# Rotation tables of the state space built inside the second MLP's weight loop on GpSimd, in the attention's old query space

## The reference

```
mag = exp(lr * dt)
ar, ai = mag * cos(li * dt), mag * sin(li * dt)
...
_, _, xr, xi = lax.associative_scan(combine, (a_r, a_i, bu_r, bu_i), axis=1)
y = einsum('blgp,ghp->blgh', xr, c_re) - einsum('blgp,ghp->blgh', xi, c_im)
```

```
x = x + mod_x[5] * sqrelu_mlp(rms_norm(x, g) * (1 + mod_x[4]) + mod_x[3], mlp_w1, mlp_w2)
```

## Time and profile before

| | us |
|---|---|
| median of 3 timed runs | 2764.59 |
| lowest, highest | 2762.73, 2766.24 |
| the profiled execution, device time | 2760.31 |
| its span in the trace | 2758.5 |
| PE busy in the span | 2454.7 (89%) |
| GpSimd busy in the span | 1125.4 (41%) |

### The profile page before, as it was taken

One profiled execution on the slowest core, in us unless ns is written; L12 is line 12 of the kernel. 1 busy time (PEld: TensorE's weight loads), 2 busy tenths in 40 slices (PEclk: granted clock), 3 DMA queues, 4 the chain that ended last, 5 costly groups with the idle time before them and its releaser, 6 DMA issues.

```text
span 2758.5 us, 31907 instructions
## 1 busy us (share of the span) xinstructions
PE 2454.7 (89%) x11622; PEld 1975.0 (72%) x11622; DVE 1513.6 (55%) x2034; ACT 956.7 (35%) x1494; POOL 1125.4 (41%) x843
## 2 busy tenths in 40 slices
PE   5999768899999997679989999897878788899999
PEld 5888657788888886556768888676534465688887
DVE  6756756755555544988552122479379444452523
ACT  3312222512121224457552233443333343432322
POOL 1433003344444432358634444345764131344444
PEclk6999879999999998889999999999989899999999
DMA  5333103232333331321122323132200020232323
GB/s 223 115 102 127 39 8 115 84 114 101 112 111 102 114 99 39 102 54 41 56 77 92 99 92 96 62 108 84 92 0 0 31 73 27 69 107 91 99 92 107
DMA packets 68821, 231.68 MB, mean 84 GB/s; under 512 B 8048, under 2 KB 10992, under 8 KB 68592
## 3 DMA queue, kind: packets, MB, share of 16 engines
q1 hardware_dynamic: 68720, 230.35, 25.8%
HBM read 219.57 MB, written 2.10 MB: 80 GB/s over the span
## 4 chain that ended last, share of the span: by engine, by line
PE 57%; issue 15%; DVE 13%; POOL 10%; ACT 3%; DMA 1%; SPq 0%; POOLq 0%; DVEq 0%; ACTq 0%
PE PS L640 41%; POOL HL L517 9%; PE PS L658 6%; DVE RD L2242 2%; PE PS L677 1%; PE PS L609 1%; PE PS L901 1%; DVE ZZ L2396 1%; DVE SM L2226 1%; PE PS L1160 1%; PE PS L783 1%; PE PS L1042 1%; PE PS L1077 1%; DVE STATE L2081 1%; PE PS L786 1%
## 5 line engine op out<-in xcount | busy, mean ns | idle before, releaser
L517 POOL TENSOR_TENSOR HL<-RAW,HL 128x512 fp32r<-128x512 f32 x614 | 905.0, 1497 | 1502.3 <-ACT HL L1205 1502.0
L640 PE MATMUL PS<-HA,HL 128*128 128x512 f32 (+1 forms) x2592 | 557.3, 368 | 18.3 <-DVE V L2007 5.1
L640 PE MATMUL PS<-HID,HL 128*128 128x512 f32 (+1 forms) x2832 | 565.6, 362 | 0.0
L640 PE MATMUL PS<-HB,HL 128*128 128x512 f32 (+1 forms) x2592 | 542.8, 362 | 0.0
L640 PEld LDWEIGHTS PS<-HID,HL 128*128 128x128 f32 x2832 | 478.8, 188 | 85.4
L640 PEld LDWEIGHTS PS<-HA,HL 128*128 128x128 f32 x2592 | 444.4, 190 | 111.4 <-issue 32.3
L640 PEld LDWEIGHTS PS<-HB,HL 128*128 128x128 f32 x2592 | 442.8, 189 | 77.5
L1205 ACT ACTIVATE HL<-RAW 128x1024 fp32r<-128x1024 f32 x307 | 323.0, 1053 | 495.5 <-PE PS L640 385.5
L1859 DVE CUSTOM_DVE_ANT_0 ADJ<-ADA,CB 128x1024 f32<-128x1024 f32 x160 | 267.8, 1674 | 8.8 <-DVE X L1781 2.7
L1781 DVE SCALAR_TENSOR_TENSOR X<-PS,MOD,X 128x256 f32<-128x256 f32 (+1 forms) x120 | 75.7, 658 | 335.2 <-PE PS L640 317.1
L658 PE MATMUL PS<-HA,HL 128*128 128x256 f32 (+1 forms) x576 | 136.1, 399 | 69.6 <-DVE HA L1762 49.2
(11 more groups left out here) (372 smaller groups left out, 2779.1 us busy)
## 6 DMA issues: line engine op xcount, KB each, us to landing
RAW<-wstream SPq DMA_DIRECT2D x307, 512.0 KB, 3.5
ADA<-adastream SPq DMA_DIRECT2D x80, 512.0 KB, 3.6
EARLY<-adastream SPq DMA_DIRECT2D x16, 512.0 KB, 14.4
QB<-QH SPq DMA_DIRECT2D x32, 128.0 KB, 2.3
X<-x_in SPq DMA_DIRECT2D x8, 384.0 KB, 6.8
QC<-QL SPq DMA_DIRECT2D x16, 128.0 KB, 2.3
out<-X SPq DMA_DIRECT2D x8, 256.0 KB, 2.3
X<-mem SPq DMA_DIRECT2D x1, 1024.0 KB, 12.3
```

The source lines that it names most:

```text
L517: a = pool.tensor_tensor(HL[:, t % RING, 1, half], RAW[:, t % RAW_RING, half], HL[:, t % RING, 0, half].bitcast(F32), ALU.subtract)
L640: mm = pe.matmul(bank(t % 2, r), w[:, wp, k * P:(k + 1) * P], a[:, ap, lo:hi], start=(k == 0 and (wp, ap) == (0, 0)), stop=(k == nk - 1 an ...
```

## The change

The doubling is cut in two halves, `turn_products` and `turn_sums`. Each of the 14 halves is placed ahead of one `low` of tiles 157 to 170 (`T_TURNS` = `T_U2` - 24), written out instead of looped: products(i), low of tile 157+2i, sums(i), low of tile 158+2i. The tables move to the space of `CB` (`cb_at`), which the attention used for `QC` and `RC`, and `PX` moves to a space behind the MLP's buffers. GpSimd waits for the attention's last low part (`att_low` at 8) ahead of the tables; its wait for tile 214 moves to the first turning of chunk 0. `turns_ready` is raised within the MLP.

```diff
+T_TURNS = T_U2 - 24
...
-        TC = sb("TC", [P, KC, P], offset=ha_at)
-        TS_ = sb("TS_", [P, KC, P], offset=ha_at + 4096)
+        TC = sb("TC", [P, KC, P], offset=cb_at)
+        TS_ = sb("TS_", [P, KC, P], offset=cb_at + 4096)
...
-        PX = sb("PX", [P, 2, KC, 64], offset=ha_at + 40960)
+        PX = sb("PX", [P, 2, KC, 64], offset=arena + 67840)
...
-            lows(T_OUT1 + AHEAD, T_OUT2 + AHEAD)
+            lows(T_OUT1 + AHEAD, T_TURNS)
...
-            pool.wait_ge(S("tile_done"), T_OUT2)
...
+            def turn_products(wide):
                 wc = prm(R_W7C).unsqueeze(2).to_broadcast([P, KC, wide])
                 ws = prm(R_W7S).unsqueeze(2).to_broadcast([P, KC, wide])
                 c0, s0 = TC[:, :, 0:wide], TS_[:, :, 0:wide]
+                tt(TC[:, :, wide:2 * wide], c0, wc, ALU.mult)
+                tt(PX[:, 0, :, 0:wide], s0, ws, ALU.mult)
+                tt(TS_[:, :, wide:2 * wide], s0, wc, ALU.mult)
+                link(tt(PX[:, 1, :, 0:wide], c0, ws, ALU.mult))
+
+            def turn_sums(wide):
                 c1, s1 = TC[:, :, wide:2 * wide], TS_[:, :, wide:2 * wide]
...
+                tt(c1, c1, PX[:, 0, :, 0:wide], ALU.subtract)
+                link(tt(s1, s1, PX[:, 1, :, 0:wide], ALU.add))
...
+            pool.wait_ge(S("dve_once"), ONCE["prm_ready"])
+            pool.wait_ge(S("att_low"), ATT_HEADS // 2)
...
+            for i in range(7):
+                turn_products(2 ** i)
+                low(T_TURNS + 2 * i)
+                turn_sums(2 ** i)
+                low(T_TURNS + 2 * i + 1)
             pool.sem_inc(S("turns_ready"), 1)
+            lows(T_TURNS + 14, T_OUT2 + AHEAD)
...
                     pool.wait_ge(S("bt_ready"), 4)
+                    pool.wait_ge(S("tile_done"), T_OUT2)
```

More of the change, by code:

```diff
@@ L560, in _ @@
                 c0, s0 = TC[:, :, 0:wide], TS_[:, :, 0:wide]
-                c1, s1 = TC[:, :, wide:2 * wide], TS_[:, :, wide:2 * wide]
-                x0, x1 = (PX[:, i, :, 0:wide] for i in range(2))
-                tt(c1, c0, wc, ALU.mult)
-                tt(x0, s0, ws, ALU.mult)
-                tt(s1, s0, wc, ALU.mult)
-                link(tt(x1, c0, ws, ALU.mult))
-                tt(c1, c1, x0, ALU.subtract)
-                link(tt(s1, s1, x1, ALU.add))
+                tt(TC[:, :, wide:2 * wide], c0, wc, ALU.mult)
[3 more added lines that the diff above has]
+            def turn_sums(wide):
+                c1, s1 = TC[:, :, wide:2 * wide], TS_[:, :, wide:2 * wide]
+                tt(c1, c1, PX[:, 0, :, 0:wide], ALU.subtract)
+                link(tt(s1, s1, PX[:, 1, :, 0:wide], ALU.add))
                 tt(prm(R_T0), prm(R_W7C), prm(R_W7C), ALU.mult)
@@ L574, in _ @@
                 link(tt(prm(R_W7S), prm(R_T2), prm(R_T2), ALU.add))
-                wide *= 2
+            pool.wait_ge(S("dve_once"), ONCE["prm_ready"])
+            pool.wait_ge(S("att_low"), ATT_HEADS // 2)
+            pool.memset(TC[:, :, 0:1], 1.0)
+            pool.memset(TS_[:, :, 0:1], 0.0)
+            pool.tensor_copy(prm(R_W7C), prm(R_COS))
+            link(pool.tensor_copy(prm(R_W7S), prm(R_SIN)))
+            for i in range(7):
[3 more added lines that the diff above has]
+                low(T_TURNS + 2 * i + 1)
             pool.sem_inc(S("turns_ready"), 1)
+            lows(T_TURNS + 14, T_OUT2 + AHEAD)
             def seg(x):
```

7 lines of the change are left out of this document (removed).

## The result

The changed kernel takes 2743.27 us (median of four runs, 2741.28 to 2748.50) against 2765.41 us (2762.73 to 2768.55, four runs) for the kernel before on the same chip: ratio 0.9924, 95% interval 0.9909 to 0.9939. It is 22.1 us faster. The profiled execution took 2741.28 us, with a span of 2739.5 us, 19.0 us less than the profiled one of before.

A forecast was written before the change was run, and what follows sets the result against it. GpSimd's tables behind tile 214 were taken to bound the first two rounds. The terms 10.5 + 1.8 - 0 = 12.3 us took the median from 2764.6 to 2752.3 us, range 2748 to 2757.

The forecast's parts named there:

- First term: Round 1: with the tables gone, head 1's softplus comes at 2003.46 in place of 2013.95, 10.5 us.
- Second term: Scans of chunk 0: the first pair no longer meets chunk 1's turning, 0.73 in place of 2.55 us, 1.8 us.
- The rhythm: Alternating rounds of 18.1 and 16.2 us: a changed start could shift one, 1.9 us either way, in the range only.
- Third term: Second MLP: table halves fit GpSimd's idle time or the low parts' lead, costing nothing, bounded by 0 and 0.8 us.
- slip point of 8.9 us: Tile 170 in the MLP: PE waits for each us its low part slips past 8.9 us (1700.20 less 1691.31).
- rival 3: Slower: GpSimd becomes the bound of the MLP at the low parts of tiles 157 to 173, 2779.1 us; chance 0.03.
- the forecast's own span: Whole kernel: least gain 8.9 us, most 15.2 us, before the range was widened to 2748 and 2757.
- Rival 1: Round 1: slow PE, or scans meeting a turning after all, leave 10.5 us or a little less, 2754.1; chance 0.15.
- Rivals 2 and 4: 2: gain mostly given back in later rounds or projection, 2760, chance 0.06; 4: BU held the first turning, under 0.01.

The follow-up runs named there:

- the pair with the shortened MLP: Kernel before and changed kernel, both without the context matmuls for fourteen of sixteen tiles per first-MLP quarter: 2647.05 us and 2632.18 us.
- the tables twice: Changed kernel with the whole table building done again at the old place behind tile 214: 2756.35 us, ratio 1.0000 to the kernel before.
- the run with twelve multiplies: Changed kernel with twelve linked, unread GpSimd multiplies added ahead of the low part of tile 170: 2755.18 us, ratio 0.9989 to the kernel before.

## Why the prediction came out too small

The rounds of all profiled executions of the two programs, the pair with the shortened MLP included:

| | before (4) | change (5) | mean difference | forecast |
|---|---|---|---|---|
| softplus 0 to 1 | 27.4 28.9 27.8 29.2 | 17.0 15.3 15.3 16.9 15.3 | 12.4 | 10.5 |
| softplus 1 to 2 | 18.0 18.1 18.0 18.0 | 16.2 16.9 17.0 17.0 16.2 | 1.4 | 1.8 |
| softplus 2 to 7 | 86.1 87.9 84.5 90.1 | 85.3 86.9 87.0 87.0 85.3 | 0.9 | 0 |
| rounds | 131.5 134.9 130.4 137.4 | 118.5 119.1 119.2 120.9 116.8 | 14.6 | 12.3 |

The last value of each kernel is from the shortened pair, which widens the difference: without it the mean differences are 11.9, 1.3, -0.4 and 12.8 us.

**What bounds the kernel before.** Right. GpSimd's tables were the bound of the first two rounds: with them doubled in the old place the gain is zero, with 19 of their 27 us gone it is nearly whole.

**First term, 10.5 us.** The mechanism is right: the turning started with BU, ACT's copy came behind the weights of head 0, and the next late thing was the logits of head 1. It was mis-sized: 12.4 us on the average, 11.9 without the shortened pair. Two readings of a single trace failed. The first is the logits' time, 1995.5 to 2000.19, "nothing in that depends on GpSimd". That is so, but they came behind 20 sums at PE's lower clock, 6.39 us in place of 4.71. In the kernel before that cost nothing, since the tables were later still. The trace of before held a slack of 1.7 us that is a cost only where it is no longer slack, and I read the time with it. In the first profile of the change the sums took 6.39 us again, and the interval, forecast at 2003.46 - 1986.56 = 16.90 us, was 16.99; in three of the other four it is 15.3. The mean, 16.0, is 0.9 us under the forecast. The second is the interval of before, 27.39 us, the shortest of its four; their mean, 28.35, is another 1.0 us. The agreement of the first profile with the forecast was thus in part luck: all six profiles of the variants that build no more than the last doubling behind tile 214 have 16.9 to 17.0 us in this interval.

**Second term, 1.8 us.** Confirmed in its place: the first pair of scans took 0.73 us in all five profiles. Its size hung on PE's clock, and there the prediction was right in only two of five. It said that the clock should stay up once the gap is closed, which gives 16.2 us from head 1 to head 2, and had 16.9 as the other value. The window from 2000 to 2020 had 1.00 in place of 0.57, but the sums stand ahead of it: those of head 1 took 4.71 us in two profiles, with an interval of 16.2, and 6.28 to 6.39 us in three (granted clock 0.76 in 1996 to 2003), with an interval of 16.9 to 17.0, and DVE waited 1.7 to 2.9 us for ACT. The mean is 1.4 us. The Trainium skill's rule that the slow clock is the default and activity lifts it ("TensorE: Matmul & The Clock Gate", section "What's actually happening") agrees with the 4.87 us of twelve matmuls behind a wait of 9.7 us and 2.91 of the next twelve. That closing the gap would keep the clock up in round 1, which the prediction drew from the rule, did not hold in those three profiles.

**The rhythm.** I had put 1.9 us either way into the range. The later intervals are 0.9 us shorter in the mean and scatter by 5 us among executions of the kernel before alone.

**Third term, 0.** Right for the tiles. PE had no wait for a low part; the tables twice gave the ratio 1.0000. The lead at tile 170 shrank to 4.0 us, where 1700.20 - 1695 = 5.2 was forecast: one of the two sums took 1.73 us in place of 1.26 and the five small instructions 1.73 in place of 0.96, beside DVE instructions and part of the 2 us allowed for such meetings. The slip point of 8.9 us was confirmed by the run with twelve multiplies. The price of rival 3 was too low by the clock: past the slip point one pays the wait and 2.0 to 2.8 us for the matmuls behind it. A thing that I did not have: the norm sum behind this MLP ran at a granted clock of 0.50 in the change, 2.90 us for its four matmuls against 1.53 at the same place in the kernel before, and the stretch is 1.4 us longer. Over the five profiles of the change these matmuls took 2.90 us three times and 1.53 twice, and the stretch is 370.6 to 372.2 us in four and 369.2 in one. The cause stays open; it is not the table work alone, since the tables twice and the turning behind the rotations have them in the MLP too and 1.53 us there.

**The total, and the step that failed most.** It is the step from the three terms to the range, which took everything outside the rounds as unchanged and repeatable, and put 1.3 and 1.4 us on the two ends for it. The three terms, at 14.6 us by the table (12.8 without the shortened pair), lie in the forecast's own span of 8.9 to 15.2 us. The measured 22.1 do not, and of the 19.0 us between the two profiled spans 6.7 are in the first MLP, to which the sum gave nothing. The spread of 1.8 us came from three runs of before. The runs of before in three later groups, each on one chip, spread over 11 to 17 us (2749.5 to 2764.1 in one, 2754.8 to 2771.4 in another), their medians lay from 2757.97 to 2764.36 us, and stretches that the change does not touch moved by up to 6.7 us in the profiles. By these numbers, which were not there at the time, the range had to be wider to the fast side by some 5 us. Why this comparison gave 22.1 us, and not the 13 to 15 of the rounds, stays open.

**What stays open.** Whether the first MLP's pace is part of the measured 22.1, 19.5 and 15.2 us. In the profiled executions it is 6.7 us of the difference. The timed executions don't show their stages, and the examples above say that they can have another pace than the profiled one. Without the alternation 14.9 us are left, about what the rounds have by the table. I take 13 to 15 us for the effect of the change: the rounds show it, and so do the shortened kernels. The rest, 4 to 6 us of the mean of 18.9 us, I take for the pace and scatter, which is an inference. What sets the pace was not found, and no mechanism is known by which tables moved behind it could set it.

**The rivals.** Rival 1, the first term alone, had two conditions. The scans did not meet the turning; the slow PE in round 1 was there in three of five profiles, and cost 0.7 us of the second term and not all of it. Rivals 2 and 4 did not occur: the later rounds gave nothing back, and the turning did start as soon as BU was filled. Rival 3 needs at tile 170 a piece nearly twice as long as the longest that the change inserts (the sums of width 64 with the small instructions, 4.8 us in the profile).

## What to carry to other kernels

Work that nobody waits for was free in a stretch with full PE as long as each piece was shorter than the lead of what it delays; cut it by the steps of that stretch, and compare each piece with the time from the delayed item's end to its use. If such work leaves a stretch where it was the bound, the gain is what the others could do at their best, not what they did while they waited: look whether the next in line was slowed in the trace at no cost then, and in several profiles, since its speed may differ among them. And before a range is made from one profile and a few runs, compare stretches that the change can't touch; here they differ by more than a third of the gain.

## What the runs showed of the hardware

- Matmuls of 512 and 256 columns in alternation run at one of two paces, 8.32 or 8.48 us for a tile of 48, at full granted clock and without waits, and keep it for a quarter of the MLP. The first MLP takes 556.8 to 566.0 us in the profiles here, by the number of slow quarters.
- DVE's instructions with two SBUF operands and GpSimd's lengthen each other: a rotation 1.64 to 1.76 us beside a turning and 0.69 alone, a scan pair 1.80 to 2.78 and 0.73 to 0.86, a step of 128x1 1.04 and 0.16, and GpSimd's multiply 1.60 to 1.73 and 1.26. The Trainium skill says that they contend, by an exclusive lock ("SBUF — State Buffer", section "Who interferes with whom"). The run that moves the turning behind the rotations shows what that is worth: 7 to 8 us of the rounds for a changed wait.
- PE behind a gap of 9.7 us took 4.87 us for twelve matmuls that take 2.88 at full clock; behind 15.5 us, 7.74 us for twenty-one that take some 4.9. A wait cost more than its length.
- The same matmuls of the same program, behind the same gap of 1.90 us, do not always have the same clock: the 20 sums of head 0 took 6.39, 4.71, 4.71 and 6.31 us in four profiles of the change, with a granted clock of 0.76, 1.00, 1.00 and 0.76 in 1980 to 1987 us.
